# Every fourth weighted one-hot made by GpSimd instead of VectorE in the gates' stage of a decoder-and-PEER kernel

## The reference, cut to what matters

```python
eid = e1 * N_KEYS + e2
gate = jax.nn.softmax(sc, axis=-1)
act = jax.nn.gelu(jnp.einsum('chkd,cd->chk', exp_u[eid], xc))
out = jnp.einsum('chk,chkd->cd', gate * act, exp_v[eid])
```

## Time and profile before

| | us |
|---|---|
| median of 3 runs | 1684.84 (1683.5 to 1684.86) |
| the profiled execution, its time | 1682.85 |
| its span | 1681.1 |
| VectorE busy over the span | 1342.0 (80%) |
| TensorE busy over the span | 1604.8 (95%) |
| GpSimd busy over the span | 561.0 (33%) |
| gates' stage, first one-hot to last matmul | 590.3 to 726.9 |

### The profile page before, as it was taken

The page is one execution under the profiler, slowest core; times in us unless marked ns, Lnnn a source line. Parts: engine busy times, 40 slices in busy tenths (PEclk is TensorE's granted clock), DMA queues, the critical chain, the costliest instruction groups (busy, mean ns, idle before and its releaser), DMA issues.

```text
span 1681.1 us, 25034 instructions
## 1 busy us (share of the span) xinstructions
PE 1604.8 (95%) x8955; PEld 1418.6 (84%) x8955; DVE 1342.0 (80%) x2723; ACT 665.3 (40%) x1088; POOL 561.0 (33%) x539
## 2 busy tenths in 40 slices
PE   7999987999899899969999999999999999999998
PEld 5777665879898899959999999999999999998886
DVE  5788455459999899957888888888888888889886
ACT  5322545333323368843333333333333333333334
POOL 1000000046465600024444445444444444445420
PEclk9999999999999999989999999999999999999999
DMA  8321822143221348888999999999999999999884
GB/s 287 120 73 57 322 76 70 51 143 89 76 76 31 108 132 250 251 297 312 338 333 351 348 339 337 353 348 348 334 346 352 333 337 350 353 336 360 324 314 139
DMA packets 164432, 411.59 MB, mean 245 GB/s; under 512 B 15504, under 2 KB 76462, under 8 KB 162894
## 3 DMA queue, kind: packets, MB, share of 16 engines
q1 hardware_dynamic: 118229, 242.20, 42.6%
q0 software_dynamic: 46080, 167.79, 26.7%
HBM read 375.34 MB, written 33.24 MB: 243 GB/s over the span
## 4 chain that ended last, share of the span: by engine, by line
PE 65%; DVE 10%; POOL 3%; issue 3%; DMA 1%; SPq 1%; ACT 0%; DVEq 0%; POOLq 0%; ACTq 0%
PE bank L1561 31%; PE bank L1513 26%; PE bank L1542 4%; PE bank L1398 3%; POOL hit L1779 2%; DVE ef L2007 1%; PE bank L1448 1%; DMA u<-in_uT 1%; SPq L1340 1%; DVE i L1943 1%; DVE sc L1937 1%; DVE i L1934 1%; DVE placed L2108 1%; DVE ci L1953 1%; DVE cand L1955 1%
## 5 line engine op out<-in xcount | busy, mean ns | idle before, releaser
L1561 PE MATMUL bank<-v_parts,p_high 128*128 128x512 f32 x1404 | 434.2, 390 | 0.7 <-DVE p_low L1913 0.7
L1513 PE MATMUL bank<-h_high,u_high 128*128 128x384 f32 x1024 | 349.5, 341 | 22.1 <-DVE u_low L1913 21.4
L1513 PE MATMUL bank<-h_high,u_low 128*128 128x384 f32 x1024 | 347.0, 339 | 0.0
L1513 PE MATMUL bank<-h_low,u_high 128*128 128x384 f32 x1024 | 346.5, 338 | 0.0
L1827 POOL DMA_INDIRECT rows<-in_u_rows,row_u x160 | 198.4, 1240 | 383.1 <-DVE dots L2141 218.4
L1561 PEld LDWEIGHTS bank<-v_parts,p_high 128*128 128x128 f32 x1404 | 262.1, 188 | 52.6 <-issue 1.8
L1827 POOL DMA_INDIRECT rows<-in_v,row_u x160 | 211.5, 1322 | 241.8 <-DVE y L2151 168.4
L1913 DVE TENSOR_TENSOR u_low<-u,u_high 128x1024 fp32r<-128x1024 f32 x133 | 164.4, 1242 | 155.8 <-ACT u_high L1651 155.5
L1561 PE MATMUL bank<-v_parts,p_low 128*128 128x512 f32 x702 | 275.0, 392 | 0.0
L1513 PEld LDWEIGHTS bank<-h_high,u_high 128*128 128x128 f32 x1024 | 195.1, 191 | 28.4 <-DVE u_low L1913 23.2
L1717 ACT CAST p_high<-gel 128x384 fp32r<-128x384 f32 x128 | 65.9, 515 | 378.7 <-DVE gel L2129 361.6
(11 more groups left out here) (255 smaller groups left out, 2490.4 us busy)
## 6 DMA issues: line engine op xcount, KB each, us to landing
u<-in_uT SPq DMA_DIRECT2D x128, 512.0 KB, 5.5
vv<-in_v SPq DMA_DIRECT2D x117, 512.0 KB, 5.4
gate<-gates_kept SPq DMA_DIRECT2D x30, 768.0 KB, 8.8
gates_kept<-staged SPq DMA_DIRECT2D x11, 2048.0 KB, 9.7
w_in_sb<-in_w_in SPq DMA_DIRECT2D x9, 1024.0 KB, 8.4
wq<-in_w_q SPq DMA_DIRECT2D x16, 512.0 KB, 3.6
ckT<-in_ckT SPq DMA_DIRECT2D x4, 1536.0 KB, 13.2
cv<-in_cv SPq DMA_DIRECT2D x8, 768.0 KB, 11.6
```

Source lines behind the costliest of these rows:

```text
L1513: ins = pe.matmul(a_ps[q % 2][:, 0:DT], x[:, k], y, start=(k == 0 and n == 0), stop=(k == KT - 1 and n == 2))
L1561: ins = pe.matmul(y_ps[2 * (i - 1) + half][:], x[:, b, of], y[:, part], start=(t == 0 and n == 0), stop=(t == NK - 1 and n == 2))
```

## The change

Twelve of the 48 weighted one-hots, those of batches 3, 7, 11 and so on to 47, the last of each block, are made by GpSimd. `here` gets a second buffer, so that VectorE can go on to the next batch's second one-hot while GpSimd reads the last. TensorE, and VectorE before it writes a buffer of `here` again, wait for the semaphore of the engine that makes the batch.

```diff
@@
+PLACED_BY_POOL = range(3, BATCHES, 4)
@@ tiles and semaphores
-        here = sb("here", [P, TB // 2, NK, 2], BF16)
+        here = sb("here", [P, 2, TB // 2, NK, 2], BF16)
+        placed_by_pool = sem("placed_by_pool")
@@ helpers
+        def placed_ready(n):
+            by_pool = sum(m in PLACED_BY_POOL for m in range(n + 1))
+            return (placed_by_pool, by_pool) if n in PLACED_BY_POOL else (placed_made, n + 1 - by_pool)
+
+        def weighted_one_hot(engine, n):
+            w = wT[:, n * TB:(n + 1) * TB].rearrange("p (g t o) -> p g t o", t=2, o=1)
+            return engine.tensor_tensor(placed[:, n % HOTS].rearrange("p (g t) k -> p g t k", t=2),
+                                        here[:, n % 2].rearrange("p g k t -> p g t k"),
+                                        spread(w, [P, TB // 2, 2, NK]), ALU.mult)
@@ TensorE, per row of 384
-                pe.wait_ge(placed_made, n + 1)
+                pe.wait_ge(*placed_ready(n))
@@ GpSimd, ahead of the row gathers
+            pool.wait_ge(slot_taken, 1)
+            for n in PLACED_BY_POOL:
+                pool.wait_ge(g_done, TB * (n - HOTS + 1))
+                pool.wait_ge(here_made, n + 1)
+                weighted_one_hot(nc.gpsimd, n).then_inc(placed_by_pool, 1)
@@ VectorE, per batch
-                wait(dve, placed_made, n)
-                nc.vector.tensor_tensor(here[:], counts, for_batch(e2b, n), ALU.is_equal).then_inc(here_made, 1)
-                wait(dve, g_done, TB * (n - HOTS + 1))
-                dve.wait_ge(here_made, n + 1)
-                w = wT[:, n * TB:(n + 1) * TB].rearrange("p (g t o) -> p g t o", t=2, o=1)
-                nc.vector.tensor_tensor(placed[:, n % HOTS].rearrange("p (g t) k -> p g t k", t=2),
-                                        here[:].rearrange("p g k t -> p g t k"),
-                                        spread(w, [P, TB // 2, 2, NK]), ALU.mult).then_inc(placed_made, 1)
+                if n >= 2:
+                    dve.wait_ge(*placed_ready(n - 2))
+                nc.vector.tensor_tensor(here[:, n % 2], counts, for_batch(e2b, n), ALU.is_equal).then_inc(here_made, 1)
+                if n not in PLACED_BY_POOL:
+                    wait(dve, g_done, TB * (n - HOTS + 1))
+                    dve.wait_ge(here_made, n + 1)
+                    weighted_one_hot(nc.vector, n).then_inc(placed_made, 1)
```

## The result

The changed kernel took 1687.45 us (median of 13 runs) against 1683.45 us for the kernel before (13 runs). The ratio is 1.0029, 95% interval 1.0022 to 1.0037: slower by about 4.9 us (the means, 1688.06 and 1683.18, differ by that; the medians differ by 4.0). The forecast had the right sign and the wrong size, +8.9 us, and 1687.45 lies just under the range of 1688 to 1702. The profiled execution took 1685.33 us (span 1683.5).

What follows compares the result with a forecast made beforehand. VectorE's unbroken chain was taken to bound the stage, level with TensorE in blocks 1 to 8. Ten products at +0.74 us and two at +1.1 gave +9.6, less 0.7 is +8.9: 1684.84 becomes 1693.7 us, range 1688 to 1702.

Steps and rivals of the forecast that it cites:

- VectorE's unbroken chain sets the end of the stage: From batch 3 on VectorE runs without a break to the last product, and the stage ends when its chain ends.
- A faster VectorE gains nothing in blocks 1 to 8: There TensorE needs 11.32 us a block and VectorE 11.25, so only the last ten batches, some 25 us, are VectorE's alone.
- 1.33 us saved per product: VectorE's time from a second one-hot to its next instruction falls from 1.93 to 0.60 us without the product.
- the hole: Gap of 0.19 us ahead of VectorE's product, waiting for its one-hot's result: 0.79 us start to start against 0.60.
- The collision: Two-tensor operations of VectorE and GpSimd don't run together; VectorE stands until 0.13 us before GpSimd's record ends.
- I take 2.39: same element count, float output: Duration of GpSimd's product, 2.39 us, taken from its subtractions of two float 128x1024 tensors.
- the bound of 2.03: Lower bound in us for GpSimd's product, from `hit` at 1.83 ns an element plus 0.15 us fixed.
- There I let GpSimd in: GpSimd starts in VectorE's 0.19 us gap, making VectorE's next product 2.07 us late, net +0.74 us for each of ten.
- +1.1 each: Cost in us of the first product, batch 3, and of the last, batch 47, which differ from the ten between.
- -0.7 us given back: With the last block 0.74 us longer, the first loads of V are out before the stage ends, saving 0.7 us.
- If the stage grows less than 5 us with these durations, TensorE hid it: Sign for TensorE hiding the loss (7%, 1686.7 us), given GpSimd's `placed` of about 3.4 us and VectorE's of 3.3.
- The rule of the Trainium skill: GpSimd would enter after the single running `hot_b`; VectorE would lose 0.93 us each time, the sum being +11.

Runs made afterwards that it cites:

- last3: The changed kernel with only batches 39, 43 and 47 multiplied by GpSimd; 1684.83 us, ratio 1.0007 to the kernel before.
- half: The changed kernel with every second batch from 3 on, 23 products, multiplied by GpSimd; 1691.34 us, ratio 1.0052 to the kernel before.
- none: The changed kernel with no product on GpSimd, only the second buffer of `here`; 1683.65 us, ratio 1.0003 to the kernel before.
- leftout: The changed kernel with the twelve products made by nobody, so part of the gates is missing; 1680.08 us, ratio 0.9978 to the kernel before.
- turned: The changed kernel with all products on VectorE, two buffers, second one-hot made before the first; 1679.69 us, ratio 0.9976 to the kernel before.
- again: The changed kernel, but VectorE makes all 48 products and GpSimd remakes twelve into an unread place; 1701.97 us, ratio 1.0114 to the kernel before.
- fill: VectorE makes all 48 products; GpSimd runs twelve memsets in place of useless products; 1683.4 us, ratio 1.0002 to the kernel before.
- forms: VectorE makes all 48 products; GpSimd runs twelve useless operations of 128x1024 in several operand forms; single time 1702.31 us.
- turned_pool: The changed kernel with the second one-hot made before the first and twelve products on GpSimd; 1680.08 us, ratio 0.9981 to the kernel before.

## Why the forecast was right in sign and wrong in size

- **VectorE's unbroken chain sets the end of the stage**: right. It took the whole loss block by block (11.64 - 11.27 = 1.70 - 1.33), and `last3`, `half` and `none` lie on the same line.
- **A faster VectorE gains nothing in blocks 1 to 8**: right from the third on, wrong for the first two. `leftout` and `turned` gained 2.0 and 1.4 us in those two, and only 1.3 and 1.2 us in the last ten batches, of which alone something was expected. For a slower VectorE, as in the change, it makes no difference.
- **1.33 us saved per product**: right. The next batch's `hot_b` starts 0.60 us after `here`, and `turned` shows that 0.19 of the 1.33 was the hole and not the product.
- **The collision**: right, and shown by `again` and `fill`. VectorE went on 0.14 us before GpSimd's record ended (612.71 + 2.38 - 0.68 = 614.41 against 612.34 + 2.21 = 614.55), where 0.13 was put down.
- **"I take 2.39: same element count, float output"**: this is the step that failed. It took 1.90. That is 0.49 us too much in each of twelve products, 5.9 us of the sum, and also below the bound of 2.03, so that the low end of the range was too high. The row that I took is of two float tensors of full size; `forms` shows that a spread factor takes 0.48 us off. `hit` in the earlier trace rows had the closest form, a factor spread (over 16 elements), and it gave the lowest of the three figures, 2.03 us; I used it as a bound only, and the fixed part of 0.15 us that I took off its 0.617 came from another form.
- **"There I let GpSimd in"** (the hole ahead of VectorE's product): wrong. GpSimd got its turn right after the `hot_b` that was running, where VectorE has no hole to give. VectorE lost 1.70 us in place of the 1.58 that 1.90 us at the hole would have cost: 0.12 us for ten products, +1.2 us.
- The first and the last product cost +0.56 us (VectorE's `hot_b` of batch 4, issued at 600.87 with a record of 1.99 us where its own is 0.69, went on at 602.17, 13.28 us into the stage; before it was 603.04, 12.72 us into it) and +0.70 us (TensorE started batch 47 at 728.39 - 725.61 = 2.78 us after the last `here`, before 2.08) where +1.1 each was put down: mostly the same 0.49 us.

With the two corrections the sum is 10 x (1.70 - 1.33) + 0.56 + 0.70 = 4.96 us, and the stage grew by 4.96.

- **The base**: the forecast stood on a median of 3 runs, 1684.84 us; over 13 runs the kernel before takes 1683.45. Without these 1.4 us the measured time would have lain inside the range, near its low end.

- **"-0.7 us given back"**: near in size by luck, for the reason is wrong. The loads of V were not out before the stage's end. They came 0.85 us after it (731.29 less 730.44), and before it was 0.52 (727.43 less 726.91). The next load of U was issued 12.54 us after the stage's end in both (at 739.45 and 742.98). The `u_low` of the loop that follows at 771 us did come 1.1 us sooner after the last matmul. Timelines of before and of the change:

```profile
771.13 1.22 DVE L1913 TENSOR_TENSOR u_low<-u,u_high 128x1024 fp32r<-128x1024 f32 x1 [1.58 <-ACT u_high L1651]
```

```profile
773.55 1.22 DVE L1932 TENSOR_TENSOR u_low<-u,u_high 128x1024 fp32r<-128x1024 f32 x1 [1.57 <-ACT u_high L1664]
```

That is 44.22 us after 726.91, and 43.11 us after 730.44. But 0.98 of the 1.11 us lie in one product of TensorE between them. The chain that ended last, before and after the change:

```profile
754.46 6.81 PE bank L1513 x24
```

```profile
757.86 5.83 PE bank L1526 x24
```

TensorE had idled 13.24 and 13.10 us ahead of it. Its matmuls came 0.32 us apart (the level of 1.2 GHz) for 15 of them before and for 9 after, then 0.17 us apart (2.4 GHz); the granted clock over the stretch was 0.62 and 0.74. In `none` this product took 6.44 us and in `last3` 7.12, so as far as these traces show it goes with the execution and not with the change. From the stage's end to the end of the span there are 954.2 us before, 953.1 after the change, 954.0 in `none` and 955.5 in `last3`: no run shows that the longer last block gave anything back. Only in `again` and `forms` were the loads out before the stage's end (747.17 against 749.10, 746.67 against 748.62), and there the rest was 3.0 and 2.3 us shorter (951.2 and 951.9); that the loads caused it is argued, not shown. Without this term the stage's +4.96 us stand beside the 4.9 us of the runs, whose interval goes from 3.7 to 6.2.

- **"If the stage grows less than 5 us with these durations, TensorE hid it"**: it grew by 4.96, but not with these durations: 2.21 and 2.38 us were measured where 3.4 and 3.3 were put down. TensorE hid nothing, every middle block is 0.37 us longer.

The rule of the Trainium skill (SBUF — State Buffer, section SBUF: two separate sides) that was weighed, an exclusive lock held for an instruction, told the turn rightly where I didn't: after the one instruction that was running. The traces agree in all ten middle products of the change (2.21 us each) and in `again`, where GpSimd started 0.02 us ahead and VectorE's product stood until it was done. They disagree in the 4.62 us of the earlier trace rows and the 4.55 and 2.82 us in `turned_pool`, where more than one instruction passed. When GpSimd is let in and when not stays open.

## What to carry to other kernels

Before work is moved from VectorE to GpSimd, look for a row in which both run two-input operations at once: if VectorE's record is as long as GpSimd's, and VectorE sets the pace, moving pays only if VectorE stands for less than it saves. Here it stood for 1.70 us (GpSimd's 1.90 less 0.2) to save 1.33. Price an operation by a row of the same form of operands and not only of the same size. And look at short gaps ahead of an instruction that needs its neighbour's result: putting an independent instruction between them gave 0.24% here, as much as leaving the twelve products out altogether.

## What the runs showed of the hardware that was not expected

- GpSimd's time for 1024 elements per partition depends on the form: 2.38 us for two float tensors, 2.14 with one of them bf16 in memory order, 2.37 with bf16 at a step of two, 1.90 with a factor spread over 128 elements, 1.04 for a copy from bf16.
- A one-input copy on GpSimd (1.04 us) holds VectorE's two-input product for 0.85 us, a memset of 1.81 us not at all.
- VectorE needs 0.257 us for each compare-and-multiply of 128x128 float with two numbers per partition.
- Waiting for the result of the instruction just before costs VectorE 0.19 us against going on with an independent one (0.79 against 0.60). In batches 0 to 2 of the kernel before, whose product doesn't wait for `g_done` as well, it is 0.12 (591.65 - 590.93 = 0.72); no run takes the two apart in the later batches.
